# Feed-forward projections with the split input stacked: one 512-column product for a weight tile's high part

## The reference, cut to what matters

```python
def swiglu(t, w_in, w_out):
    a, b = jnp.split(t @ w_in, 2, axis=-1)      # w_in: 1024 x 5632
    return (jax.nn.silu(a) * b) @ w_out         # w_out: 2816 x 1024

x = x + g2 * swiglu(modulate(rmsnorm(x, norm2_g[i]), sh2, sc2), ffn_w_in[i], ffn_w_out[i])
# rmsnorm(x, g) = x * rsqrt(mean(x*x) + 1e-6) * g;  modulate(x, shift, scale) = x * (1 + scale) + shift
```

## Time and profile before

| | us |
|---|---|
| median of 3 runs | 1093.45 (1092.46 to 1093.78) |
| the profiled execution, whole | 1093.67 |
| its span, first to last instruction | 1091.9 |
| PE busy | 1038.2 (95%) |
| PEld busy | 965.1 (88%) |
| DVE busy | 784.3 (72%) |
| ACT busy | 507.2 (46%) |
| mean granted TensorE clock | 0.988 of full |

### The profile page before, as it was taken

One profiled execution on the slowest core, in us unless ns is written; L12 is line 12 of the kernel. 1 busy time (PEld: TensorE's weight loads), 2 busy tenths in 40 slices (PEclk: granted clock), 3 DMA queues, 4 the chain that ended last, 5 costly groups with the idle time before them and its releaser, 6 DMA issues. The chain is left out here.

```text
span 1091.9 us, 18245 instructions
## 1 busy us (share of the span) xinstructions
PE 1038.2 (95%) x7726; PEld 965.1 (88%) x7726; DVE 784.3 (72%) x1177; ACT 507.2 (46%) x700; POOL 0.7 (0%) x6
## 2 busy tenths in 40 slices
PE   4899999799999999998999999999999999999995
PEld 2689875699999999998999999999987998888984
DVE  3689759668788787887985656568736569786565
ACT  3623238554434334324443434445347556547462
POOL 0000000000000000000000000000000000000000
PEclk9899999999999999999999999999999999999998
DMA  9769541038898987566646666554754053445020
GB/s 368 269 210 337 185 173 39 2 117 292 307 317 291 312 289 237 196 222 228 242 165 221 201 234 219 176 175 149 234 183 139 7 192 127 162 166 198 1 78 38
DMA packets 116545, 210.15 MB, mean 192 GB/s; under 512 B 4251, under 2 KB 78193, under 8 KB 116465
## 3 DMA queue, kind: packets, MB, share of 16 engines
q1 hardware_dynamic: 115716, 206.81, 55.1%
q10 hardware_dynamic: 748, 2.18, 0.5%
HBM read 207.92 MB, written 1.05 MB: 191 GB/s over the span
## 5 line engine op out<-in xcount | busy, mean ns | idle before, releaser
L980 DVE TENSOR_TENSOR low<-raw,high 128x2048 fp32r<-128x2048 f32 (+2 forms) x147 | 328.1, 2234 | 159.8 <-ACT high L582 159.4
L582 ACT ACTIVATE high<-raw 128x2048 fp32r<-128x2048 f32 (+2 forms) x147 | 272.9, 1866 | 215.2 <-PE PS L1569 113.3
L1652 PE MATMUL PS<-hH,high 128*128 128x258 f32 x896 | 221.9, 284 | 4.5 <-ACT high L582 1.9
L1653 PE MATMUL PS<-hL,high 128*128 128x258 f32 x896 | 220.3, 283 | 0.0
L1652 PEld LDWEIGHTS PS<-hH,high 128*128 128x128 f32 x896 | 169.8, 189 | 6.4 <-issue 2.8
L1653 PEld LDWEIGHTS PS<-hL,high 128*128 128x128 f32 x896 | 168.7, 188 | 0.1
L1671 PE MATMUL PS<-hH,low 128*128 128x258 f32 x896 | 126.2, 283 | 0.3
L1671 PEld LDWEIGHTS PS<-hH,low 128*128 128x128 f32 x896 | 115.6, 189 | 1.4 <-DVE low L980 1.4
L1567 PE MATMUL PS<-gH,high 128*128 128x256 f32 x352 | 98.4, 280 | 0.0
L1568 PE MATMUL PS<-gL,high 128*128 128x256 f32 x352 | 98.4, 280 | 0.0
L1569 PE MATMUL PS<-gH,low 128*128 128x256 f32 x352 | 98.2, 279 | 0.0
(11 more groups left out here) (315 smaller groups left out, 1935.3 us busy)
## 6 DMA issues: line engine op xcount, KB each, us to landing
raw<-in_ffn_w_in SPq DMA_DIRECT2D x44, 1024.0 KB, 6.2
ada_raw<-in_ada_w SPq DMA_DIRECT2D x82, 512.0 KB, 5.4
raw<-in_ffn_w_out SPq DMA_DIRECT2D x22, 1024.0 KB, 6.2
raw<-in_na_w_in SPq DMA_DIRECT2D x16, 1024.0 KB, 5.5
raw<-in_da_wqkv SPq DMA_DIRECT2D x12, 1024.0 KB, 8.7
raw<-in_sc_w_in SPq DMA_DIRECT2D x12, 1024.0 KB, 6.3
raw<-in_ple_w_gate SPq DMA_DIRECT2D x8, 1024.0 KB, 4.8
raw<-in_mla_w_in SPq DMA_DIRECT2D x7, 1024.0 KB, 5.3
```

What stands on the lines that cost most here:

```text
L582: nc.scalar.activation(high[s][:, 0:width(u)], raw[s][:, 0:width(u)], ACT.Copy).then_inc(high_ready, 1)
L980: V_.tensor_tensor(low[s][:, 0:w], raw[s][:, 0:w], high[s][:, 0:w].bitcast(F), ALU.subtract).then_inc(low_dve, 1)
L1652: MM(PS[:, b + c, 0:SEQ + 2], high[s][w(j, c)], hH[:, j, 0:SEQ + 2], start=j == 0, stop=False)
L1653: MM(PS[:, b + c, 0:SEQ + 2], high[s][w(j, c)], hL[:, j, 0:SEQ + 2], start=False, stop=False)
```

## The change

- `oH` and `oL` become the two halves of one tile `oHL`, 128 x 2 x 8 x 256.
- From step 3 on (`PAIRED = 3`), both feed-forwards take their input from `oHL`, which holds the high and low part of the whole input, with `rstd`, scale and shift applied. A tile of `high` is multiplied by both parts in one product of 512 columns (two runs of 256 that lie 2048 numbers apart), which fills a bank; a tile of `low` is multiplied by the high part in one product of 256 columns, added onto the bank's first half (`paired_features`).
- DVE takes such banks out with a `tensor_reduce` that adds the two halves of the bank (`both_parts`). The shift copy falls away, and silu and the gating are one instruction each over 512 elements instead of two over 256.
- The input is made in steps 0 and 1: at the end of step 0 DVE multiplies `XT` by `rstd` into `paired` (the room of `XN`); at the end of step 1 ACT applies scale and shift with eight Identity instructions in place, waits for itself, and makes `oH` by a copy of 2048 columns; at the end of its step 1 DVE waits for that and makes `oL` by a subtraction. PE waits for it (`paired_low`) at the start of step 3.
- Steps 0 to 2 remain as before, and so do the convolution and all else.

```diff
@@ -59,6 +59,7 @@
 VALUE_BANK = (6, 7)
 ZV_BANK = ((0, 1), (2, 3), (4, 5), (6, 7))
 Z_BANK = ((3, 1), (2, 3))
+PAIRED = 3
 UP_BANK = (4, 6, 0, 4, 2, 0, 4, 6)
 
 
@@ -248,8 +249,8 @@
         with ExitStack() as s:
             mqn = sb("ml_qT", [P, KC, SEQ], F, s)
             mkn = sb("ml_kT", [P, KC, SEQ], F, s)
-        oH = sb("oH", [P, KC, SEQ], R)
-        oL = sb("oL", [P, KC, SEQ], R)
+        oHL = sb("oHL", [P, 2, KC, SEQ], R)
+        oH, oL = oHL[:, 0, :, :], oHL[:, 1, :, :]
         XT = sb("XT", [P, KC, SEQ])
         rstd = sb("rstd", [P, SEQ])
         wide = [sb(f"wide{i}", [P, SEQ]) for i in range(4)]
@@ -334,6 +335,7 @@
         Zg = X
         by_feature = "p t (k n) -> p (t k) n"
         XT_squares = XN[:, :, :].rearrange(by_feature, n=SEQ)
+        paired = XN[:, :, :].rearrange(by_feature, n=SEQ)
         XG_squares = X[:, :, :].rearrange(by_feature, n=SEQ)
         PT_proj = gates[:, :, :].rearrange(by_feature, n=SEQ)
         c_squares = gates[:, :, :].rearrange(by_feature, n=SEQ)
@@ -392,6 +394,9 @@
         conv_staged = sem("conv_staged")
         head_gated = sem("head_gated")
         hid_low = sem("hid_low")
+        paired_scaled = sem("paired_scaled")
+        paired_high = sem("paired_high")
+        paired_low = sem("paired_low")
         out_ready = sem("out_ready")
         vz_copied = sem("vz_copied")
         heads_copied = sem("heads_copied")
@@ -715,12 +720,14 @@
                 behind(first["da_out"] + k)
             close(first["da_out"] + 3, SCALE2, SHIFT2)
 
-            def ffn_phase(u0):
+            def ffn_phase(u0, scale, shift):
                 for i in range(FSTEPS):
                     ua = u0 + (3 * i - 1 if i else 0)
                     seen.next(a_taken)
-                    for c in range(2):
+                    for c in range(2 if i < PAIRED else 0):
                         ins = nc.scalar.activation(sil[:, c, :], ta[:, c, :], ACT.Silu, bias=shifts[:, c:c + 1])
+                    if i >= PAIRED:
+                        ins = nc.scalar.activation(sil[:, :, :], ta[:, :, :], ACT.Silu)
                     ins.then_inc(silu_ready, 1)
                     behind(ua)
                     if i < FSTEPS - 1:
@@ -731,8 +738,16 @@
                         behind(ua + 1)
                     if 1 <= i < FSTEPS - 1:
                         behind(ua + 2)
-
-            ffn_phase(first["ffn0"])
+                    if i == 1:
+                        seen.next(paired_scaled)
+                        for c in range(KC):
+                            ins = nc.scalar.activation(paired[:, c, :], paired[:, c, :], ACT.Identity,
+                                                       scale=mod[:, scale, c:c + 1], bias=mod[:, shift, c:c + 1])
+                        ins.then_inc(act_step, 1)
+                        seen.next(act_step)
+                        nc.scalar.activation(oH[:, :, :], paired[:, :, :], ACT.Copy).then_inc(paired_high, 1)
+
+            ffn_phase(first["ffn0"], SCALE2, SHIFT2)
             close(first["sc_in"] - 1, 6 + SCALE1, 6 + SHIFT1)
 
 
@@ -751,7 +766,7 @@
                 behind(first["sc_out"] + k)
             close(first["sc_out"] + 3, 6 + SCALE2, 6 + SHIFT2)
 
-            ffn_phase(first["ffn1"])
+            ffn_phase(first["ffn1"], 6 + SCALE2, 6 + SHIFT2)
 
             def highs(u, scale):
 
@@ -1223,6 +1238,10 @@
 
                 return V_.tensor_tensor(dst[:, :, :], PS[:, b:b + 2, 0:SEQ], rstd[:, :].unsqueeze(1).to_broadcast([P, 2, SEQ]), ALU.mult)
 
+            def both_parts(dst, b):
+
+                return V_.tensor_reduce(dst[:, :, :], PS[:, b:b + 2, :].rearrange("p c (h n) -> p c n h", h=2), AX.X, ALU.add)
+
             def shift_column(b, c):
                 return PS[:, b + c, SEQ:SEQ + 1]
 
@@ -1234,13 +1253,18 @@
                 for i in range(FSTEPS):
                     ua = u0 + (3 * i - 1 if i else 0)
                     v.wait_ge(blocks_done, block_end[ua])
-                    V_.tensor_copy(shifts[:, :].unsqueeze(2), PS[:, 4:6, SEQ:SEQ + 1])
-                    scaled(ta, 4).then_inc(a_taken, 1)
+                    if i < PAIRED:
+                        V_.tensor_copy(shifts[:, :].unsqueeze(2), PS[:, 4:6, SEQ:SEQ + 1])
+                        scaled(ta, 4).then_inc(a_taken, 1)
+                    else:
+                        both_parts(ta, 4).then_inc(a_taken, 1)
                     behind(ua - 1 if i == 0 else ua)
                     v.wait_ge(blocks_done, block_end[ua + 1])
-                    link(scaled(tb, 6))
+                    link(scaled(tb, 6) if i < PAIRED else both_parts(tb, 6))
                     seen.next(silu_ready)
-                    for c in range(2):
+                    if i >= PAIRED:
+                        ins = V_.tensor_tensor(gated[:, :, :], tb[:, :, :], sil[:, :, :], ALU.mult)
+                    for c in range(2 if i < PAIRED else 0):
                         ins = V_.scalar_tensor_tensor(gated[:, c, :], tb[:, c, :], shift_column(6, c), sil[:, c, :], ALU.add, ALU.mult)
                     ins.then_inc(g_ready, 1)
                     if i == 0:
@@ -1253,6 +1277,11 @@
                         behind(ua + 1)
                     if 1 <= i < FSTEPS - 1:
                         behind(ua + 2)
+                    if i == 0:
+                        V_.tensor_tensor(paired[:, :, :], XT[:, :, :], rstd[:, :].unsqueeze(1).to_broadcast([P, KC, SEQ]), ALU.mult).then_inc(paired_scaled, 1)
+                    if i == 1:
+                        seen.next(paired_high)
+                        V_.tensor_tensor(oL[:, :, :], paired[:, :, :], oH[:, :, :].bitcast(F), ALU.subtract).then_inc(paired_low, 1)
 
             ffn_phase(first["ffn0"])
             close(first["sc_in"] - 1, GATE2, 6 + SCALE1, 6 + SHIFT1, early=True)
@@ -1671,6 +1700,25 @@
                         last = MM(PS[:, b + c, 0:SEQ + 2], low[s][w(j, c)], hH[:, j, 0:SEQ + 2], start=False, stop=j == KC - 1)
                     last.then_inc(blocks_done, 1)
 
+            def paired_features(u, b):
+
+
+                s = u % RING
+
+                def w(j, c):
+                    return (slice(None), slice(j * 256 + c * P, j * 256 + (c + 1) * P))
+
+                pe.wait_ge(high_ready, u + 1)
+                for c in range(2):
+                    claim(b + c)
+                    for j in range(KC):
+                        MM(bank(b + c), high[s][w(j, c)], oHL[:, :, j, :], start=j == 0, stop=False, skip_group_check=True)
+                    if c == 0:
+                        unit_ready(u)
+                    for j in range(KC):
+                        last = MM(bank(b + c, SEQ), low[s][w(j, c)], oH[:, j, :], start=False, stop=j == KC - 1, skip_group_check=True)
+                    last.then_inc(blocks_done, 1)
+
             def shared_features(u, b, opening=False):
 
                 s = u % RING
@@ -1874,12 +1922,20 @@
                 for i in range(FSTEPS + 1):
                     if i < FSTEPS:
                         ua = u0 + (3 * i - 1 if i else 0)
-                        two_features(ua, 4, i == 0)
+                        if i < PAIRED:
+                            two_features(ua, 4, i == 0)
+                        else:
+                            if i == PAIRED:
+                                seen.next(paired_low)
+                            paired_features(ua, 4)
                         owed(a_taken, 4, 5)
                         if i == 0:
                             sum_of_squares()
                         behind(ua)
-                        two_features(ua + 1, 6)
+                        if i < PAIRED:
+                            two_features(ua + 1, 6)
+                        else:
+                            paired_features(ua + 1, 6)
                         owed(g_ready, 6, 7)
                     if i >= 1:
                         seen.next(hid_low)
```

## The result

The changed kernel takes 1099.45 us (median of 4 runs, 1098.18 to 1100.06), the kernel before 1093.62 in the runs beside it. The ratio is 1.0051, 95% interval 1.0039 to 1.0063. The profiled execution of the changed kernel is its fastest run, 1098.18 us with a span of 1096.4.

A forecast was written before the change was run, and what follows sets the result against it. PE was taken to bound the kernel, except that DVE's queue sets ffn0's end. Terms: +4.9 us ffn0, +0.8 half clock, -4.1 ffn1, sum +1.6 us, giving 1095.0 us; range 1089.5 to 1099.5.

The forecast's parts named there:

- B: Rival on DVE's reductions: strided pairs cost more than 1.22 us; at 1.38, 2.6 us more, 1097.6 us; chance 0.12.
- half clock in ffn0: PE's half clock after waiting 6.7 us before ffn0's last output: 1.6 to 2.6 us lost, 0.8 of it showing.
- C: Rival on DVE's reductions: they cost near 0.69 us, so ffn0 keeps gain too: 1087.7 us; chance 0.12.
- DVE's step in ffn0: Steps 3 to 10: reductions at 1.22 us make DVE's step 0.54 us longer, 17.80 or 17.25 us.
- The making in ffn0: Steps 0 and 1: making the split input delays DVE; PE waits 2.0 and 0.5 us, ffn0 ends 4.9 later.
- The product of 512 columns: PE's paired product at 0.2267 us: each tile product saves 0.0162 us, 4.1 us per feed-forward.
- the other end of the bounds: Paired product priced as two of 256 columns, 0.2354 us: gain only 1.9 us per feed-forward.
- ffn1: the step that failed: DVE's idle time in ffn1 hides the making and longer sums, so PE's full 4.1 us saving shows.
- waits of PE in ffn1: Sign listed as showing the forecast wrong; it expected PE to have no waits in the second feed-forward.
- DVE as the bound of ffn0: DVE's queue sets ffn0's end, 4.9 us later, so PE's 4.1 us saving there is worth nothing.
- Rival E: PE's pairing saves less than a product's fixed cost, 0.7 or 1.9 us in ffn1: 1098.5 or 1097.3; chance 0.07.
- Rival D: PE's half-clock stretch at 516 falls elsewhere: 2.6 us back, 1092.4; chance 0.05, plus 0.04 with cheaper DVE.

The follow-up runs named there:

- e3: Changed kernel with the halves of the split input interleaved by chunk, so a paired product's moving operand is one run of 512 numbers: 1099.13 us.
- e2: Changed kernel with DVE's wait for the copy and its subtraction moved from the end of step 1 to step 2: 1097.62 us.
- e5: Kernel before with the change in the second feed-forward alone, DVE's subtraction moved to step 2: 1090.31 us.
- e4: Changed kernel with the reduction over a bank's halves replaced by a copy of the first half, leaving out high weights x low input: 1096.92 us.
- e8: Changed kernel with paired products from step 4 on in ffn0, step 3 in ffn1, and the subtraction in step 2 in both: 1094.70 us.
- e11: Changed kernel, pairing from the fourth step on in both feed-forwards, each piece of the making placed where its engine waits anyway: 1089.42 us.
- e12: As e11, but ffn0's steps 3 to 10 use three products of 256 columns per tile, without sums over halves or products by the root: 1087.22 us.
- e1: Changed kernel with the split input still made and waited for, but the old products, shift columns and bank reading: 1102.27 us.
- e10: As e9, but paired products begin at step 4 in ffn0, and in ffn1 DVE makes the input with the subtraction in step 2: 1094.75 us.
- e6: As e5, but three products of 256 columns per tile from step 3 on, ACT and DVE reading the banks directly: 1092.37 us.
- e9: Changed kernel, pairing from the fourth step on in both feed-forwards, with DVE's multiplication and subtraction of the making on GpSimd: 1097.66 us.

## Why the prediction held, and where its steps were wrong

The forecast was 1095.0, the time 1099.45, 0.05 us inside the upper edge of the range. That the range held is luck: its upper part was there for dearer reductions (B), which didn't come, and the 5.8 us that ffn1 missed by had no place in it. The total missed by less only because 0.8 us forecast for half clock in ffn0 didn't come and the medians differ by 0.6 us less than the two feed-forwards do in the traces. The lower edge, 1089.5, doesn't lie half of the way to C either, which would be 1091.4. The forecast was right on the side of ffn0 and wrong on ffn1.

**DVE's step in ffn0: right.** Reductions 1.22 us as taken (rivals B and C, dearer or cheaper, are out; 1.218 us for `ta` and 1.217 for `tb`, eight each), DVE's steps 17.78 and 17.23 against 17.80 and 17.25. From step 3 on DVE never waits for PE, and `ta` of step 10 starts at 418.66, which is 420.3 on the scale of before (+1.61), forecast 420.4.

**The making in ffn0: right in size and in cause, wrong on where PE waits.** `ta` of step 2 came 20.5 us behind that of step 1, forecast 20.5; PE's waits at step 3 were 1.86 and 0.18 against 2.0 and 0.5. From the start of step 1's a unit to the last output it is 430.55 - 246.01 = 184.54 us against 427.38 - 247.62 = 179.76: +4.8, forecast +4.9. But I had it as one wait of 6.7 us ahead of the last output; it was 1.17. PE had lost the time earlier: 1.60 for bank 7 and about 1.6 at half clock from 290.97. Of the stretch's +4.76, -2.7 is the products' saving and 6.6 the waits and the half clock named so far; some 0.9 lies in rows a little longer behind waits (2.10 and 1.21 for 2.02 and 1.10), which I didn't place one by one. The end was right, and not by luck, because it hangs on DVE's queue, wherever PE waits.

**The product of 512 columns: mis-sized.** Taken at 0.2267 from the row at 59.93; measured 0.2325. The attention's projection, where that row stands, has the fastest products of this width. The trace of before had the other price too, 168 products between these two rows, 0.2324 apart:

```profile
783.14 0.48 PE L1567 MATMUL PS<-high,hH 128*128 128x512 f32 x1
...
821.95 0.39 PE L1569 MATMUL PS<-high,hL 128*128 128x512 f32 x1
```

The saving per tile product is then 0.0104 us, 2.7 us per feed-forward and not 4.1. e3 shows that the reason isn't the gap in the operand, which was my explanation for the other end of the bounds, and the 168 products show that it isn't the pairing. Why the attention's are faster stays open. That 1.4 us of the miss comes from choosing the cleanest row.

**ffn1: the step that failed.** "The 2.2 us multiplication, the wait for ACT and the subtraction fit": they fit in DVE's idle time summed over the step, but not where they stood. The subtraction waited 3.38 us for ACT at the head of the queue, and behind it stood the section's read, for which PE waited 2.64 us; 1.5 us at half clock followed. -4.1 forecast, +1.66 measured: of the 5.8 between them, 1.4 is the product, 2.6 the wait, 1.5 the half clock (588.97 to 592.35 for sixteen products that take 1.9), and 0.3 isn't placed. e2 and e5 show it: with the subtraction one place later the 185.25 us of the changed kernel become 180.96 and 180.97, under the 183.59 of before. I named "waits of PE in ffn1" as a sign against me without looking which of DVE's readers PE needs next. In the trace of before nobody waits for the section's read (L973), so no list of waits shows it. The kernel's text does: the columns lie in bank 7, and PE claims bank 7 for the second half of the b unit.

**The clock: in the wrong place.** I forecast half clock behind the wait ahead of the last output of ffn0, 0.8 us of it visible. That wait was 1.17 us and the granted clock is 1.00 over 430.50 to 433.50, so this term came to nothing. Half clock came inside ffn0 behind the section, where DVE's queue covers it, and in ffn1 behind 2.64 us, where nothing does and the 1.5 us show.

**DVE as the bound of ffn0.** The argument that PE's saving is worth nothing there was right for the kernel as built (e4: cheaper sums give 2.0 us back) but too strong: PE ran its 16.87 and 18.67 us steps there with the dear sums, in the changed kernel as in e8 and e11. What DVE holds is the end of the phase. There it was late already in the kernel before, as I had read from the earlier trace rows, and e12 puts that at 1.9 us.

**Rival E**, pairing saves less than a product's fixed cost, named the time nearest to the one measured (1098.5 or 1097.3), but not for its reason: the pairing saves 2.6 us in e5, more than E's 0.7 or 1.9, and the rest of E's time was ffn0's 5.7. **Rival D** is out: the half-clock stretch in the convolution is still there behind the same wait (granted 0.63 over 519.6 to 522.6), and the row between the feed-forwards moved by 0.29 us.

## What to carry to other kernels

An engine's idle time per step is no cover for new work by itself: ask at which place of its queue it is idle, and whose read stands behind the new instruction. The same change, products and making, was +5.8 us with the making at the end of the steps and -4.2 us with each piece where its engine waited for its partner. Before you price a gain of 5% on a product, take the width's rows as a group and not the cleanest one; and if an input can be made ready once, look first at what it lets the other engines drop (e12), then at how many products it merges.

## What the runs showed of the hardware

- Half clock behind a wait isn't certain. The same work and the same wait for bank 7 in ffn1 were followed by a granted clock of 0.54 over 588.97 to 592.30 in the changed kernel, by half clock from about 1.1 us after the wait in e4, and by none in e1. The changed kernel, e4, then e1:

```profile
588.97:592.30 3.33, 3.33 (x16) 0.54 0.00 0
```

```profile
590.20:591.20 1.00, 1.00 (x8) 1.00 0.00 0
591.20:593.50 2.30, 2.30 (x13) 0.50 0.00 0
```

```profile
590.10:593.50 3.40, 3.40 (x28) 1.00 0.00 0
```

  PE's instructions in ffn1 ahead of these waits were the same in all three. What decides it stays open. Behind 5.80 us of waiting in e2 the clock was 0.58 over 6.9 us. In ffn0 it fell right behind the section's sixteen one-column products in the changed kernel, where PE had rested 1.86, 0.18 and 0.18 us in the 9 us before them, and in e10, where the timeline has only two gaps of about 0.1 us there. The same products without a rest ahead of them (e5) were followed by full clock. e10, then e5:

```profile
291.00:294.00 3.00, 3.00 (x18) 0.59 1.11 389
```

```profile
288.00:294.00 6.00, 6.00 (x50) 1.00 0.99 321
```

- Products of fp32r started 0.118 us apart at 256 columns, 0.120 at 258 and 0.2325 at 512 (0.2324 in one part of the kernel before, 0.2267 in another). One product of 512 columns saves only 0.004 us against two of 256 (e6).
- A GpSimd instruction from SBUF to SBUF and a DVE instruction with two SBUF operands didn't run beside each other: DVE lost 3.6 us (gating) and 2.0 us (a split) in e9, and GpSimd 1.9 us behind a split.
- A `tensor_reduce` from PSUM with a stride of 256 between its two inputs takes 1.22 us for 1024 inputs, as the reductions over neighbours do.
